# Three moves in the delta heads: key products of the next head, copies of the solved rows, and the key decays on GpSimd

## The reference, cut to what matters

```python
kb = k * beta[..., None]
a_mat = jnp.where(strict, jnp.einsum('bhncd,bhnsd->bhncs', kb, k) * decay_mat, 0.0)
lhs = a_mat + jnp.eye(CHUNK, dtype=F32)
rhs = jnp.concatenate([v * beta[..., None], kb * jnp.exp(gc)[..., None]], axis=-1)
sol = lax.linalg.triangular_solve(lhs, rhs, left_side=True, lower=True, unit_diagonal=True)
u, w = sol[..., :dv], sol[..., dv:]
qk = jnp.einsum('bhncd,bhnsd->bhncs', q, k) * decay_mat
q_dec = q * jnp.exp(gc)[..., None]
k_dec = k * jnp.exp(gc[..., -1:] - gc)[..., None]

def step(state, inp):
    qk_c, qd_c, kd_c, u_c, w_c, gl_c = inp
    v_new = u_c - jnp.einsum('bhcd,bhde->bhce', w_c, state)
    o = jnp.einsum('bhcd,bhde->bhce', qd_c, state) + jnp.einsum('bhcs,bhse->bhce', qk_c, v_new)
    state = state * gl_c[..., None, None] + jnp.einsum('bhcd,bhce->bhde', kd_c, v_new)
    return state, o
```

## Time and profile before

| what | value |
|---|---|
| median of 3 runs | 1760.26 us (1758.93 to 1760.47) |
| the profiled execution | 1758.72 us, its span 1756.9 us |
| PE busy | 1728.2 us, 98% |
| DVE, ACT, POOL busy | 63%, 46%, 16% |
| granted TensorE clock | 1.00, the upper level, 2.4 GHz |
| the delta heads | 196 to about 428 us, with a period of 27.3 us for a head |

### The profile page before, as it was taken

How to read it: one execution, slowest core, us unless ns; L and a number is a source line. 1 busy time by engine, 2 the same in 40 slices (tenths; PEclk the granted TensorE clock), 3 DMA queues, 4 the chain that set the end, 5 groups by cost and what they waited for, 6 DMA issues and landing times.

```text
span 1756.9 us, 27499 instructions
## 1 busy us (share of the span) xinstructions
PE 1728.2 (98%) x10944; PEld 1426.3 (81%) x10944; DVE 1109.5 (63%) x1604; ACT 799.7 (46%) x1352; POOL 279.5 (16%) x268
## 2 busy tenths in 40 slices
PE   8999999999999999999999999999999999999999
PEld 6888778877889988888887888889988888876777
DVE  4776377775787746757321687787746766433763
ACT  4433555453346743343543454246643445434541
POOL 2001176662000010010000243000010010101600
PEclk9999999999999999999999999999999999999999
DMA  5223100000333344242322100233354252430002
GB/s 167 84 87 116 49 14 14 2 2 2 96 99 118 108 157 144 96 138 72 96 89 80 36 13 25 72 119 99 121 181 137 89 175 83 155 96 24 25 1 72
DMA packets 103282, 147.32 MB, mean 84 GB/s; under 512 B 5153, under 2 KB 71153, under 8 KB 102912
## 3 DMA queue, kind: packets, MB, share of 16 engines
q1 hardware_dynamic: 96192, 121.45, 22.2%
q0 software_dynamic: 6976, 24.27, 4.2%
HBM read 143.61 MB, written 2.10 MB: 83 GB/s over the span
## 4 chain that ended last, share of the span: by engine, by line
PE 91%; DVE 3%; POOL 2%; ACT 1%; issue 1%; DMA 1%; SPq 0%; DVEq 0%; POOLq 0%; ACTq 0%
PE bk L305 23%; PE bk L307 23%; PE bk L306 23%; PE bk L1236 3%; PE bk L1208 1%; PE bk L1229 1%; PE bk L1218 1%; PE bk L3394 1%; PE bk L3395 1%; POOL work L1732 1%; PE bk L2530 1%; PE bk L3416 1%; POOL work L1730 1%; PE bk L2456 1%; DMA X<-in_x 1%
## 5 line engine op out<-in xcount | busy, mean ns | idle before, releaser
L284 DVE TENSOR_TENSOR wlo<-raw,whi 128x1024 fp32r<-128x1024 f32 x166 | 198.1, 1230 | 273.9 <-ACT whi L278 273.4
L305 PE MATMUL bk<-act_hi,whi 128*128 128x512 f32 (+1 forms) x880 | 323.8, 368 | 0.3 <-DVE wlo L797 0.3
L307 PE MATMUL bk<-act_hi,wlo 128*128 128x512 f32 (+1 forms) x880 | 320.8, 365 | 0.0
L306 PE MATMUL bk<-act_lo,whi 128*128 128x512 f32 (+1 forms) x880 | 320.8, 365 | 0.0
L305 PE MATMUL bk<-whi,act_hi 128*128 128x512 f32 (+1 forms) x776 | 307.7, 397 | 0.5 <-DVE act_lo L643 0.5
L307 PE MATMUL bk<-whi,act_lo 128*128 128x512 f32 (+1 forms) x776 | 306.2, 395 | 0.0
L306 PE MATMUL bk<-wlo,act_hi 128*128 128x512 f32 (+1 forms) x776 | 303.6, 391 | 0.0
L278 ACT ACTIVATE whi<-raw 128x1024 fp32r<-128x1024 f32 x166 | 168.7, 1054 | 254.7 <-PE bk L307 231.0
L305 PEld LDWEIGHTS bk<-act_hi,whi 128*128 128x128 f32 x880 | 165.7, 188 | 31.3 <-issue 1.1
L306 PEld LDWEIGHTS bk<-act_lo,whi 128*128 128x128 f32 x880 | 165.7, 188 | 29.5 <-issue 1.0
L307 PEld LDWEIGHTS bk<-act_hi,wlo 128*128 128x128 f32 x880 | 165.6, 188 | 29.4
(11 more groups left out here) (457 smaller groups left out, 3057.1 us busy)
## 6 DMA issues: line engine op xcount, KB each, us to landing
raw<-in_mlp_w SPq DMA_DIRECT2D x100, 512.0 KB, 4.2
raw<-in_a_w_in SPq DMA_DIRECT2D x32, 512.0 KB, 4.2
work<-in_mlp_w SPq DMA_DIRECT2D x28, 512.0 KB, 4.6
work<-in_w_mod POOLq DMA_DIRECT2D x24, 512.0 KB, 3.9
raw<-in_b_w_in SPq DMA_DIRECT2D x24, 512.0 KB, 3.9
raw<-in_w_in SPq DMA_DIRECT2D x14, 512.0 KB, 4.4
raw<-in_a_w_out SPq DMA_DIRECT2D x8, 512.0 KB, 4.1
raw<-in_b_w_out SPq DMA_DIRECT2D x8, 512.0 KB, 3.4
```

What stands on the lines that cost most here:

```text
L284: nc.vector.tensor_tensor(wlo[b][:, hs], src[hf][:, :], whi[b][:, hs], ALU.subtract).then_inc(w_ready, 1)
L305: nc.tensor.matmul(acc, lhs_hi, rhs_hi, start=first, stop=False, skip_group_check=True)
L306: nc.tensor.matmul(acc, lhs_hi, rhs_lo, start=False, stop=False, skip_group_check=True)
L307: return nc.tensor.matmul(acc, lhs_lo, rhs_hi, start=False, stop=last, skip_group_check=True)
```

## The change

On PE the key products of the next head move from behind the opening of level 6 to ahead of it. On DVE the first pairs move from between T and Z of level 6 to the end of level 5, behind the output norm; the first sums stay. The numbers in two waits follow from that order of `G["t"]`. At the start of a head DVE copies the solved rows ahead of scaling the key products. POOL runs both key decays before the wait for the first sums and both query decays behind it.

```diff
@@ pe_a_level_close
-                pe.wait_ge(G["t"], 14 * h + 2 * l + s + 1)
+                pe.wait_ge(G["t"], 14 * h + 2 * l + s + (3 if l == 6 and h + 1 < AH else 1))
@@ pe_a_head
             for l in range(1, LEVELS):
+                if l == 6 and more:
+                    pe_a_kk(pe, h + 1)
                 pe_a_level_open(pe, h, l)
...
                 if l == 6 and more:
-                    pe_a_kk(pe, h + 1)
                     pe_a_decay(pe, h + 1)
@@ dve_a_first_sums
-                dve.wait_ge(G["t"], 14 * h + 2)
+                dve.wait_ge(G["t"], max(2, 14 * h))
@@ dve_a_head
             if h > 0:
+                dve_a_new(dve, h - 1, 0)
                 dve_a_k(dve, h)
-                dve_a_new(dve, h - 1, 0)
...
                 if l == 6 and more:
-                    dve_a_first_pairs(dve, h + 1)
                     dve_a_first_sums(dve, h + 1)
...
                 if l == 5 and h > 0:
                     dve_a_out_norm(dve, h - 1)
+                if l == 5 and more:
+                    dve_a_first_pairs(dve, h + 1)
@@ pool_a_head
+            for d in range(2):
+                pool_a_key_decay(pool, h, d)
+            if h + 1 < AH:
                 pool.wait_ge(G["z"], 14 * h + 14)
             for d in range(2):
                 pool_a_query_decay(pool, h, d)
 
-        def pool_a_query_decay(pool, h, d):
+        def pool_a_key_decay(pool, h, d):
             pool.wait_ge(G["row_exp"], 2 * h + d + 1)
             nc.gpsimd.tensor_tensor(A[f"ke{d}"], A[f"qd{d}"], a_kn(h).rearrange("p (c s) -> p c s", c=ST), ALU.mult).then_inc(G["ke"], 1)
+
+        def pool_a_query_decay(pool, h, d):
             pool.wait_ge(G["ke"], 2 * h + d + 1)
```

## The result

The changed kernel takes 1762.77 us (median of 20 runs, 1760.66 to 1763.80) against 1760.43 us of before in the same session (20 runs): ratio 1.0013, 95% interval 1.0007 to 1.0019, some 2.3 us slower. The profiled execution took 1761.05 us, its span is 1759.3 us, the granted clock 1.00. The forecast was 1762.4 us, no change that a single measurement could tell.

A forecast was written before the change was run, and what follows sets the result against it. PE, busy 98% of the span, was taken as the bound. Head 0 +1.8 us and six middle heads +0.4 us sum to +2.2 us, a median of 1762.4 us; range 1754.5 to 1767 us.

The forecast's parts named there:

- head 0: Step into head 1: first pairs wait for POOL's pair scales; values +1.43, way behind them +0.38, together +1.8 us.
- middle head: Each step after heads 1 to 6: 0.18 later to values, 0.12 less behind them, +0.06, six times +0.4 us.
- Ahead of level 6: Key products before the opening, first pairs earlier: without disturbance values (start of `pe_a_values`) come 0.27 us earlier.
- The 0.16 for the close: End of level 6 on PE: moving the key products fills a hole, so the close comes 0.16 us earlier.
- the 0.27 at values: Start of `pe_a_values` in a middle head: 309.34 in place of 309.61 if nothing disturbs DVE's sums.
- The collision: DVE's first sums beside POOL's key decays: 1.05 us added to the sums, values 0.18 later instead of 0.27 earlier.
- Solved rows ahead of the scaling: Start of a head: scan_new waits for DVE's later scaling, starting 1.70 after values instead of 0.92, 0.78 us later.
- The wait for POOL: Level 1: PE's 0.9 us wait for query decays goes; values to close takes 4.72 instead of 4.84.
- Rival A: First sums and key decays pass without collision: together -1.1 us, 1759.2 us; chance 0.20.
- Rival B: scan_new starts on the copies, scaling costs nothing: 0.90 less behind values, -3.3 us, 1757.0 us; chance 0.20.
- Rival C: Both key decays fall ahead of or between the first sums: up to 1.05 more per head, 1768.7 us; chance 0.20.

The follow-up runs named there:

- run 2: Changed kernel with POOL's four decays back in their old order behind the wait for the first sums: 1761.69 us, ratio 1.0012 to before.
- run 4: Kernel before with only the key products and first pairs moved ahead: 1757.65 us, ratio 0.9986 to before.
- run 8: Changed kernel with scaling ahead of copies, head 0's old order, and one key decay ahead of POOL's wait: 1754.22 us, ratio 0.9966 to before.
- run 9: Kernel of run 8 with PE turning the next head's decay behind values instead of ahead: 1754.98 us, ratio 0.9961 to before.
- run 1: Changed kernel with DVE scaling the key products ahead of copying the solved rows again: 1755.45 us, ratio 0.9975 to before.
- run 6: Changed kernel with scan_new's bank 3 products first and PE's wait for the scaling only ahead of bank 7: 1757.57 us, ratio 0.9984 to before.
- run 3: Kernel before with only both key decays moved ahead of POOL's wait for the first sums: 1754.89 us, ratio 0.9972 to before.
- run 7: Changed kernel with head 0 alone in its old order of key products and first pairs: 1760.93 us, ratio 1.0006 to before.
- run 10: Kernel of run 3 with PE turning the next head's decay behind values instead of ahead: 1756.79 us, ratio 0.9977 to before.

## Why the prediction was right, step by step

The time was right: +2.2 us forecast, +2.3 measured, and nearly all of it in head 0 (1.8 forecast, 2.0 measured), with a middle head at +0.06 forecast and about 0 measured. The steps were not all right, and that the sum of a middle head came out is luck.

- *Ahead of level 6.* Wrong in size. The key products started 0.43 after the product for the row exponentials, exactly where the opening had, and not at 0.27. I had read the opening as waiting for Z, but the same 0.43 stands behind the product in both kernels, whichever group follows: the weight loads of the opening were idle 0.25 ahead of it before, those of the key products, which need no Z, 0.25 after. The 0.16 for the close was not there (close 3.69 after the product, 3.68 before), nor the 0.27 at values without a collision: runs 2, 4 and 8, in which DVE is free early, have values at 5.54 to 5.55. I had PE's turns of key and decay done at 309.3; run 9 shows that they hold values until 5.54 after the product, 309.57 on the clock of before.
- *The collision.* There, with 0.83 in place of 1.05 on the first sums (1.93 against 1.10). The two key decays stayed at 2.14 and were not longer than alone, though I had written that they would be; DVE alone paid. The 0.22 that I took too much is what I had wrong at values: the additions started 308.81 on the clock of before and not 308.99, and values came 0.02 earlier and not 0.18 later. At 0.83 the price lies just beside PE's turns of key and decay, and run 2 shows that without the collision a middle head is no shorter. In head 0, where DVE is late, it does cost, 0.5 us in run 2. The Trainium skill (SBUF — State Buffer, Who interferes with whom) has the second to issue blocked for the whole instruction of the first; the trace agrees: the first sum started behind the second key decay and waited for what was left of that one, as the last section shows, and the second sum waited for nothing.
- *Solved rows ahead of the scaling.* Right in mechanism, 0.92 in place of 0.78, as PE started 0.25 after the scaling's end and not 0.1; the bank 7 wait is shown by runs 1 and 6.
- *The wait for POOL.* Gone, as forecast. The way from values to the close came to 4.87 and not 4.72, which is the same 0.15.
- *Head 0.* Values +1.48 against +1.43, the way behind them +0.53 against +0.38. Inside the first, T behind POOL's scales took 0.98 (run 4, no collision) where I had about 0.8, and the collision 0.50 (run 2) where I had 0.65: two misses that cancel here as well.

So in a middle head two misses cancelled: 0.20 too much at values for the collision, 0.15 too little for the wait behind them. Rival A had its condition wrong, as the collision is there, and its price too: in a middle head values come at the same time with a collision or without, and only head 0 would have gained 0.5. Rival B needed scan_new to start on the copies; run 1, in which it does so, gives 0.92 a head where B had 0.90, and run 6, which makes it possible for half of the products, gives 0.64. Rival C did not come about: the first sums stayed under 2 us.

## What to carry to other kernels

Before an instruction is moved ahead of another on an engine, list every wait that the next engine's step has: the consumer of the solved rows also needed the bank that the scaling frees, and the scaling had been in a free slot. When work is moved within a stretch in which one engine has no holes, as PE at level 6 here, the end of that engine's work stays where it is, and only an engine that is late elsewhere can gain. Three edits that belong together in the mind should be timed one by one, as one of these three alone gave 5 us and the bundle lost 2. The first pass of a loop has other neighbours than the rest, and deserves its own line in the sum.

## What the hardware showed that I had not expected

- Two DVE instructions of 1.10 together became 1.93 beside two of GpSimd, which took 2.14, as in run 3, where the first sums came only at their end. Taken one by one in the changed kernel, it is the first sum alone that waits, and it waits for the second key decay, which started 0.12 ahead of it:

```profile
309.11 1.09 POOL L1735 TENSOR_TENSOR work<-work 128x512 f32<-128x512 f32 x1
309.23 1.45 DVE L1589 TENSOR_TENSOR work<-work,arena 128x256 f32<-128x256 f32 x1
```

  The key decay had 0.97 left when the sum started, and the sum took 0.82 longer than its 0.63. The rows of the other heads, taken the same way, agree: in head 1 it had 0.59 left and the sum took 0.45 longer, in head 0 it had 0.74 left and the sum took 0.60 longer: each time what was left, less about 0.15.
- In head 0 of run 7 the second key decay came 0.12 behind the first sum and not ahead of it, and then GpSimd paid as well, 1.35 in place of 1.09; the second sum, which started behind that key decay, paid 0.84:

```profile
226.36 0.65 DVE L1591 TENSOR_TENSOR arena<-arena 128x256 f32<-128x256 f32 x1
226.48 1.35 POOL L1739 TENSOR_TENSOR work<-work 128x512 f32<-128x512 f32 x1
226.84 1.47 DVE L1591 TENSOR_TENSOR arena<-arena 128x256 f32<-128x256 f32 x1
```

  Which side pays depends on the order in which they start, by a tenth of a microsecond.
- A late wait can cost PE more than its own time. Scan_new started 0.14 after the first copy's end before (310.10 + 0.29 to 310.53), and 0.25 after the scaling's end in the changed kernel (312.71 + 0.68 to 313.64); in run 6, where the wait for the scaling stands ahead of the bank 7 products alone, it was 0.05. What makes the difference is not shown.
- Four transposes of PE, 0.44 from start to start, put into a hole of 0.5 us cost 0.25 (runs 9 and 10).
